# Gate and up products of three feed-forwards: both parts of h in one 512-column matmul, half results added by VectorE, the low part of the result on GpSimd

## The chip, the cores and the metric

One core of a Trainium2 chip runs the whole program. The metric is the device time of one execution in microseconds (us); the time of a kernel is the median of its runs.

## What is computed

Two blocks, each two layers deep, over 256 tokens of width 1024, in fp32. What matters here is the feed-forward of the first block. It comes four times (before and after the mixer of each of its two layers):

```python
def swiglu(h, w_gate, w_up, w_down):
    return (jax.nn.silu(h @ w_gate) * (h @ w_up)) @ w_down
...
x = x + 0.5 * swiglu(rms_norm(x, ffn2_norm[l]), ffn2_w_gate[l], ffn2_w_up[l], ffn2_w_down[l])
```

`w_gate` and `w_up` are 1024 x 2816, `w_down` is 2816 x 1024. The second block (retention, a gated unit, two products over 16384 experts) is not touched by the change.

## The kernel before

Everything is kept transposed: x is [128 partitions, 8 chunks of the 1024 features, 256 tokens]. Every product in fp32 is made of three products of fp32r numbers. Each operand is split into a high part and a low part (`h_hi`, `h_lo`; `w_hi`, `w_lo`), and high x high, high x low and low x high are added in PSUM by TensorE (`triple`, L620 to L623).

**Weights.** They stream from HBM in *units* of 128 x 1024, two to a load of 1 MB, into three buffers `raw` (SyncE, L2315). For each unit ScalarE writes `w_hi` (L1167) and VectorE writes `w_lo` = raw - `w_hi` (L1625). There are four buffers of each (`NPAIR`), so ScalarE may write unit n only once TensorE is done with unit n - 4, and SyncE may load only once VectorE has made the `w_lo` of three loads before. Between the pairs of units lie loads of `ada_w`; VectorE multiplies each half of these by a row and sums it (L1620), which TensorE doesn't need.

**The feed-forwards.** `FFN` lists four, c = 0 to 3. The loop over f = 0 to 21 takes 128 columns of gate (unit 2f) and of up (unit 2f + 1). A unit is 8 blocks of 128 x 128 weights, one for each chunk k of h. `project` does a block as one `triple`: three matmuls of 256 columns, into one half of a PSUM bank for gate and the other for up. For f = 0 of c > 0 `project_pairs` (L676 to L682) does the same in another order. Then, in order of the queues:

- VectorE, `ffn`: the `w_lo` of unit 2f + 4 (in `pair`); `activate(f - 1)`: it waits for Silu(f - 1), multiplies gate and up (L1771), waits for `a_hi`, and writes `a_lo` = product - `a_hi` (L1773); then it waits for unit 2f + 1 and scales both halves of the bank by the row `rr` into `sg` (L1794); then the `w_lo` of unit 2f + 5.
- ScalarE, `ffn`: the `w_hi` of unit 2f + 4; `a_split(f - 1)`: it waits for the product and copies it, rounded, to `a_hi` (L1243); the `w_hi` of unit 2f + 5; it waits for the scaling of f and takes Silu of the gate half in place (L1258).

The waits are semaphores, and each engine takes its instructions strictly in this order. `sg` has two buffers, used in turn by f.

**The down product** (`out_project`) has 176 blocks of weights. It uses `high_and_low` (L631, L632): one matmul of 512 columns takes `w_hi` against `a_hi` and `a_lo` side by side and leaves the low part's product in the bank's second half; one of 256 columns adds `w_lo` x `a_hi` to the first half. VectorE adds both halves to x (L1672, then, behind a wait for its own result, L1674). In c = 3 VectorE also works out rotary angles between the steps of f (L1738 to L1763). GpSimd adds squares of x for the next norm during the down products (`add_squares`, L2271 and L2275) and does nothing in the loops over f.

Of the kernel before, what the change touches and what calls it, by code (L numbers as in the profile page):

```python
# [17 lines left out]
T = 256  # L18
D = 1024
KT = 8  # L20
# [147 lines left out]
def build(nc, a, out):  # L168
    ctx = ExitStack()
    with ctx:  # L170
# [7 lines left out]
        hh_ = sb("h_hi", [128, KT, T], FR)  # L178
        hl_ = sb("h_lo", [128, KT, T], FR)
# [130 lines left out]
        silu_done = signal("silu_done", lambda c, f: 22 * c + f + 1)  # L310
# [125 lines left out]
        def out_after(c, key, K, m):  # L436
# [9 lines left out]
            "gu": lambda c, f: (gu_scaled, gu_scaled(c, f)),  # L446
            "out": lambda q, m: (x_upd, x_upd(q, m)),
# [169 lines left out]
        def _(e):  # L617
# [41 lines left out]

            def project_pairs(q, key, n, outs, lag=2, inside=None):  # L660

                for at in range(KT + lag * (len(outs) - 1)):
                    if at == inside:
                        added_sums(q)
                        sums(q, at, at)
                        sums(q, at + 1, at + 1)
                    for z, o in enumerate(outs):
                        k = at - lag * z
                        if not 0 <= k < KT:
                            continue  # L670
                        c = slice(k * 128, (k + 1) * 128)
                        w.wait_ge(h_hi, h_hi(q, k))
                        for half in range(2):
                            wh, wl = weights(unit[key, 2 * (n + z) + half])
                            s = slice(half * T, (half + 1) * T)
                            e.matmul(o[:, s], wh[:, c], by_halves(hh_[:, k, :]), start=k == 0 and half == 0, stop=False, skip_group_check=True)  # L676
                            e.matmul(o[:, s], wl[:, c], by_halves(hh_[:, k, :]), start=False, stop=False, skip_group_check=True)
                        w.wait_ge(h_lo, h_lo(q, k))
                        for half in range(2):
                            g = unit[key, 2 * (n + z) + half]  # L680
                            wh, wl = weights(g)
                            t = e.matmul(o[:, half * T:(half + 1) * T], wh[:, c], by_halves(hl_[:, k, :]), start=False, stop=k == KT - 1, skip_group_check=True)  # L682
                            if k == KT - 1:
                                t.then_inc(used.hit(g), 1)
# [91 lines left out]
            def ffn(c):  # L776
                which, l, q = FFN[c]
                for f in range(22):
# [4 lines left out]
                    if c == 0 and f == 14:  # L783
                        bias_tiles()
                    b = take(banks, ("gu", c, f))
# [12 lines left out]
                    if c > 0 and f == 1:  # L798
                        scale_row(q)
# [4 lines left out]
                    if c == 0 and f == 1:  # L804
                        for m in (4, 5):
                            sums(q, m, m)
                    if c == 0 and f == 2:
# [346 lines left out]
        def _(e):  # L1154
# [69 lines left out]
            def ffn(c, gains):  # L1224
# [20 lines left out]
                for f in range(22):  # L1245
# [8 lines left out]
                    if f >= 1:  # L1254
                        a_split(f - 1)
                    w_hi_upto(unit[(f"{which}_gu", l), 2 * f + 1] + 1 + NPAIR)
# [352 lines left out]
        def _(e):  # L1609
# [155 lines left out]
            def ffn(c, gains):  # L1765
# [3 lines left out]
                def activate(f):  # L1769
                    w.wait_ge(silu_done, silu_done(c, f))  # L1770
                    e.tensor_tensor(sg[f % 2][:, 0], sg[f % 2][:, 0], sg[f % 2][:, 1], ALU.mult).then_inc(gu_mul.hit(c, f), 1)  # L1771
                    w.wait_ge(a_hi_done, a_hi_done(c, f))
                    e.tensor_tensor(a_lo[:, f, :], sg[f % 2][:, 0], a_hi[:, f, :].bitcast(FP), ALU.subtract).then_inc(a_lo_done.hit(c, f), 1)  # L1773

                for f in range(22):
# [18 lines left out]
                    e.tensor_tensor(as_halves(sg[f % 2]), from_halves(bank["gu", c, f]), as_halves(one(rr).broadcast_to([128, 2, T])), ALU.mult).then_inc(gu_scaled.hit(c, f), 1)  # L1794
# [454 lines left out]
        def _(e):  # L2249
# [29 lines left out]

            for l in range(L):  # L2280
                add_squares(3 * l + 1)
# [4 lines left out]
                if l == 1:  # L2286
                    w.wait_ge(x_upd, x_upd(5, 7))
                    e.dma_start(dm, a["decay"]).then_inc(decay_in.sem, 16)
                    e.dma_start(posi, a["positions_2"].partition_broadcast(128)).then_inc(pos_in.sem, 16)
                add_squares(3 * l + 3)  # L2290
# [172 lines left out]
```

## Time and profile before

| | |
|---|---|
| Median of 3 runs | 2953.95 us (2953.05 to 2957.92) |
| The profiled execution | 2955.0 us, its span 2953.2 us |
| TensorE busy | 2919.2 us (99%) |
| TensorE weight loads | 2769.8 us (94%) |
| VectorE busy | 2204.2 us (75%) |
| ScalarE busy | 1605.8 us (54%) |
| GpSimd busy | 262.5 us (9%) |
| DMA, mean | 222 GB/s |

An engine is busy while an instruction runs on it; matmuls overlap each other, so the time that one takes is the distance between two starts and not its duration. The distance of starts is the measure on the other engines too, where the end of one instruction overlaps the next. The chain of waits runs over TensorE for 79% of the span, VectorE 10%, DMA 8%, ScalarE 2%.

### The profile page before, as it was taken

What the parts mean: (1) busy time and instruction counts of PE and PEld (TensorE: products, weight loads), DVE (VectorE), ACT (ScalarE), POOL (GpSimd) and SP (SyncE); (2) the same over time, 40 slices, a digit from 0 to 9 for tenths busy, and PEclk for the clock granted to TensorE, in tenths of its full rate; (3) what the DMA queues carried; (4) which work ended last, traced back from release to release, by engine and by line L of the source; (5) the groups of instructions that cost most, each with busy time, mean ns of one, the idle gap of its engine ahead of it and who ended that gap; (6) DMA issues with size and microseconds to landing.
All of it is one profiled execution on the core that took longest, in us unless ns stands there. A gap on an engine that the chain in (4) does not pass through costs nothing.

```text
span 2953.2 us, 51905 instructions
## 1 busy us (share of the span) xinstructions
PE 2919.2 (99%) x21818; PEld 2769.8 (94%) x21818; DVE 2204.2 (75%) x3531; ACT 1605.8 (54%) x2397; POOL 262.5 (9%) x233
## 2 busy tenths in 40 slices
PE   9999999999999999999999999999999999999999
PEld 9999999999999999999999998889999999999987
DVE  6887888886788847899755557776769986555676
ACT  5575655566544455556555555556545565555554
POOL 0010001010101102730000000000147000000000
PEclk9999999999999999999999999999999999999999
DMA  7773577775278555557876667655455688666673
GB/s 250 274 262 108 186 272 271 272 281 190 92 250 288 196 171 171 174 184 268 309 237 228 221 221 252 225 188 200 170 186 186 215 308 264 228 229 226 233 250 130
DMA packets 153688, 654.51 MB, mean 222 GB/s; under 512 B 10509, under 2 KB 77649, under 8 KB 78961
## 3 DMA queue, kind: packets, MB, share of 16 engines
q1 hardware_dynamic: 97744, 584.99, 57.0%
q10 hardware_dynamic: 55296, 64.76, 6.5%
q8 instruction: 173, 2.83, 0.4%
q0 software_dynamic: 416, 1.45, 0.1%
q14 instruction: 59, 0.48, 0.0%
HBM read 616.55 MB, written 34.61 MB: 220 GB/s over the span
## 4 chain that ended last, share of the span: by engine, by line
PE 79%; DVE 10%; DMA 8%; ACT 2%; issue 1%; DVEq 0%; ACTq 0%; SPq 0%
PE ps L621 12%; PE ps L622 12%; PE ps L623 12%; PE ps L626 8%; PE ps L628 8%; PE ps L627 8%; DMA gates<-at 6%; PE ps L631 6%; DVE w_lo L1625 3%; PE ps L632 3%; PE ps L823 2%; PE ps L697 1%; PE ps L698 1%; PE ps L700 1%; DVE raw L1620 1%; ACT w_hi L1167 1%
## 5 line engine op out<-in xcount | busy, mean ns | idle before, releaser
L1625 DVE TENSOR_TENSOR w_lo<-raw,w_hi 128x1024 fp32r<-128x1024 f32 x933 | 1140.9, 1232 | 497.2 <-ACT w_hi L1167 495.6
L1167 ACT ACTIVATE w_hi<-raw 128x1024 fp32r<-128x1024 f32 x1000 | 1048.1, 1056 | 575.2 <-PE ps L623 254.0
L621 PE MATMUL ps<-h_hi,w_hi 128*128 128x256 f32 x4240 | 1177.7, 278 | 6.2 <-DVE w_lo L1625 5.4
L622 PE MATMUL ps<-h_lo,w_hi 128*128 128x256 f32 x4240 | 1168.3, 276 | 0.0
L623 PE MATMUL ps<-h_hi,w_lo 128*128 128x256 f32 x4240 | 1168.2, 276 | 0.0
L621 PEld LDWEIGHTS ps<-h_hi,w_hi 128*128 128x128 f32 x4240 | 815.8, 192 | 12.2 <-issue 6.9
L622 PEld LDWEIGHTS ps<-h_lo,w_hi 128*128 128x128 f32 x4240 | 816.1, 192 | 2.0 <-issue 0.2
L623 PEld LDWEIGHTS ps<-h_hi,w_lo 128*128 128x128 f32 x4240 | 816.3, 193 | 0.0
L626 PE MATMUL ps<-w_hi,at 128*128 128x512 f32 x1024 | 388.4, 379 | 1.6 <-DVE at L2203 1.6
L627 PE MATMUL ps<-w_lo,at 128*128 128x512 f32 x1024 | 388.1, 379 | 0.0
L628 PE MATMUL ps<-w_hi,at 128*128 128x512 f32 x1024 | 388.1, 379 | 0.0
L631 PE MATMUL ps<-at,w_hi 128*128 128x512 f32 x832 | 273.2, 382 | 1.0 <-DVE at L1971 0.6
L632 PE MATMUL ps<-at,w_lo 128*128 128x256 f32 x832 | 226.8, 273 | 0.0
L626 PEld LDWEIGHTS ps<-w_hi,at 128*128 128x128 f32 x1024 | 193.7, 189 | 27.6 <-issue 1.9
L628 PEld LDWEIGHTS ps<-w_hi,at 128*128 128x128 f32 x1024 | 193.5, 189 | 27.4
L627 PEld LDWEIGHTS ps<-w_lo,at 128*128 128x128 f32 x1024 | 193.7, 189 | 25.8
L2271 POOL TENSOR_TENSOR tmp_h<-x 128x256 f32<-128x256 f32 x50 | 44.5, 890 | 1781.5 <-DVE x L1674 1658.0
L631 PEld LDWEIGHTS ps<-at,w_hi 128*128 128x128 f32 x832 | 157.3, 189 | 23.5 <-DVE at L1971 0.9
L2257 POOL TENSOR_TENSOR w_lo<-raw,w_hi 128x512 fp32r<-128x512 f32 x128 | 162.4, 1302 | 61.5 <-ACT w_hi L1167 61.3
L1489 ACT ACTIVATE at<-ps 128x512 f32<-128x512 f32 x128 | 76.8, 600 | 158.2 <-PE ps L623 158.1
L1560 ACT ACTIVATE at<-at 128x256 fp32r<-128x256 f32 x256 | 92.1, 409 | 126.6 <-DVE at L2199 126.6
L632 PEld LDWEIGHTS ps<-at,w_lo 128*128 128x128 f32 x832 | 159.7, 192 | 0.0
(292 smaller groups left out, 3223.2 us busy)
## 6 DMA issues: line engine op xcount, KB each, us to landing
raw<-in_peer_u SPq DMA_DIRECT2D x128, 1024.0 KB, 4.9
raw<-in_peer_v SPq DMA_DIRECT2D x128, 1024.0 KB, 4.9
raw<-in_ffn_gu SPq DMA_DIRECT2D x87, 1024.0 KB, 4.9
raw<-in_ada_w SPq DMA_DIRECT2D x48, 1024.0 KB, 5.1
raw<-in_ffn_down SPq DMA_DIRECT2D x44, 1024.0 KB, 4.9
gates<-at ACTq DMA_DIRECT2D x32, 1024.0 KB, 6.2
at<-gates ACTq DMA_DIRECT2D x24, 1024.0 KB, 6.3
raw<-in_w_in SPq DMA_DIRECT2D x16, 1024.0 KB, 4.9
```

Source lines behind the costliest of these rows:

```text
L621: e.matmul(o, lhs[0], rhs[0], start=start, stop=False)
L622: e.matmul(o, lhs[0], rhs[1], start=False, stop=False)
L623: return e.matmul(o, lhs[1], rhs[0], start=False, stop=stop)
L626: e.matmul(o, lhs[0], rhs[0], start=start, stop=False, skip_group_check=True)
L627: e.matmul(o, lhs[0], rhs[1], start=False, stop=False, skip_group_check=True)
L628: return e.matmul(o, lhs[1], rhs[0], start=False, stop=stop, skip_group_check=True)
L631: e.matmul(o, lhs[0], both.rearrange("p s (a b) -> p s b a", a=2), start=start, stop=False, skip_group_check=True)
L632: return e.matmul(o[:, 0:T], lhs[1], by_halves(both[:, 0]), start=False, stop=stop, skip_group_check=True)
L1167: e.activation(whi[:, u % NPAIR, :], raw(k, half), ACT.Copy).then_inc(hi_done.hit(u), 1)
L1560: e.activation(p_hi[k % 4], R[:, (2 * n) % NRING + e2, :], ACT.Copy).then_inc(p_hi_done.hit(l, k), 1)
L1625: e.tensor_tensor(wlo[:, m % NPAIR, :], raw(k, half), whi[:, m % NPAIR, :].bitcast(FP), ALU.subtract).then_inc(w_lo_dve.hit(m), 1)
L2257: t = e.tensor_tensor(wlo[:, n % NPAIR, c], raw(k, half)[:, c], whi[:, n % NPAIR, c].bitcast(FP), ALU.subtract)
```

## The change

In c = 1, 2 and 3, for f = 1 to 21, each block of a gate or up unit becomes a `high_and_low`: `w_hi` against the high and low parts of h at once (512 columns), then `w_lo` against the high part (256 columns). For that `h_hi` and `h_lo` lie in one tensor. Gate and up now take a bank each, of which the first half holds one partial sum and the second the other. ScalarE copies the first half of both banks to `sg`; VectorE waits for that, adds the second halves, waits for its own result and scales in SBUF. ScalarE's copies come behind `a_split(f - 1)` and wait for `a_lo` of f - 2. For the same three feed-forwards `a_lo` is made by GpSimd. c = 0 stays as it was.

```diff
--- before.py
+++ after.py
@@ -175,8 +175,8 @@
             return Signal(ctx.enter_context(nc.semaphore(name)), order)
 
         x = sb("x", [128, KT, T])
-        hh_ = sb("h_hi", [128, KT, T], FR)
-        hl_ = sb("h_lo", [128, KT, T], FR)
+        h_both = sb("h_hi_lo", [128, 2, KT, T], FR)
+        hh_, hl_ = h_both[:, 0], h_both[:, 1]
         sq = sb("sq", [128, 2, T])
         tmp_h = sb("tmp_h", [128, 3, T])
         ident = sb("ident", [128, 128])
@@ -307,7 +307,11 @@
         rows_half = signal("rows_half", lambda r: r + 1)
 
         gu_scaled = signal("gu_scaled", lambda c, f: 22 * c + f + 1)
-        silu_done = signal("silu_done", lambda c, f: 22 * c + f + 1)
+        def gu_scalar(c, f, copied=False):
+
+            return f + 1 if c == 0 else 22 + 43 * (c - 1) + 2 * f + (not copied)
+
+        silu_done = signal("silu_done", gu_scalar)
         gu_mul = signal("gu_mul", lambda c, f: 22 * c + f + 1)
         a_hi_done = signal("a_hi_done", lambda c, f: 22 * c + f + 1)
         a_lo_done = signal("a_lo_done", lambda c, f: 22 * c + f + 1)
@@ -444,6 +448,7 @@
 
         evacuated = {
             "gu": lambda c, f: (gu_scaled, gu_scaled(c, f)),
+            "gj": lambda c, f, z: (gu_scaled, gu_scaled(c, f)),
             "out": lambda q, m: (x_upd, x_upd(q, m)),
             "hook": lambda n: (hook_free, hook_free(n)),
             "lam": lambda: (lam_exp, 1),
@@ -657,6 +662,14 @@
                     t = triple(o, (wh[:, c], wl[:, c]), h_part(k), k == 0, k == KT - 1)
                 t.then_inc(used.hit(n), 1)
 
+            def project_high_and_low(q, n, o):
+                wh, wl = weights(n)
+                for k in range(KT):
+                    c = slice(k * 128, (k + 1) * 128)
+                    w.wait_ge(h_lo, h_lo(q, k))
+                    t = high_and_low(o, (wh[:, c], wl[:, c]), h_both[:, :, k, :], k == 0, k == KT - 1)
+                t.then_inc(used.hit(n), 1)
+
             def project_pairs(q, key, n, outs, lag=2, inside=None):
 
                 for at in range(KT + lag * (len(outs) - 1)):
@@ -782,6 +795,13 @@
                         lambdas()
                     if c == 0 and f == 14:
                         bias_tiles()
+                    if c > 0 and f > 0:
+                        for z in range(2):
+                            b = take(banks, ("gj", c, f, z))
+                            project_high_and_low(q, unit[(f"{which}_gu", l), 2 * f + z], b)
+                            if f == 1 and z == 0:
+                                scale_row(q)
+                        continue
                     b = take(banks, ("gu", c, f))
                     if f == 0:
                         if c == 0:
@@ -795,16 +815,14 @@
                             sums(q, m, m)
                         continue
                     project(q, unit[(f"{which}_gu", l), 2 * f], b[:, 0:T])
-                    if c > 0 and f == 1:
-                        scale_row(q)
                     if c == 0 and f < 3:
                         for m in (4 * f - 2, 4 * f - 1):
                             sums(q, m, m)
                     project(q, unit[(f"{which}_gu", l), 2 * f + 1], b[:, T:2 * T])
-                    if c == 0 and f == 1:
+                    if f == 1:
                         for m in (4, 5):
                             sums(q, m, m)
-                    if c == 0 and f == 2:
+                    if f == 2:
                         scale_row(q)
                 out_project(q + 1, (f"{which}_down", l), 22, lambda i: a_hl[:, :, i, :],
                             lambda i: (a_lo_done, a_lo_done(c, i)), c, last=c == 3)
@@ -1253,6 +1271,13 @@
                     pair((f"{which}_gu", l), f)
                     if f >= 1:
                         a_split(f - 1)
+                    if c > 0 and f > 0:
+                        if f > 1:
+                            w.wait_ge(a_lo_done, a_lo_done(c, f - 2))
+                        for z in range(2):
+                            w.wait_ge(*unit_after((f"{which}_gu", l), 2 * f + z))
+                            t = e.activation(as_halves(sg[f % 2][:, z:z + 1]), from_halves(bank["gj", c, f, z][:, 0:T]), ACT.Copy)
+                        t.then_inc(silu_done.hit(c, f, True), 1)
                     w_hi_upto(unit[(f"{which}_gu", l), 2 * f + 1] + 1 + NPAIR)
                     w.wait_ge(gu_scaled, gu_scaled(c, f))
                     e.activation(sg[f % 2][:, 0], sg[f % 2][:, 0], ACT.Silu).then_inc(silu_done.hit(c, f), 1)
@@ -1769,8 +1794,9 @@
                 def activate(f):
                     w.wait_ge(silu_done, silu_done(c, f))
                     e.tensor_tensor(sg[f % 2][:, 0], sg[f % 2][:, 0], sg[f % 2][:, 1], ALU.mult).then_inc(gu_mul.hit(c, f), 1)
-                    w.wait_ge(a_hi_done, a_hi_done(c, f))
-                    e.tensor_tensor(a_lo[:, f, :], sg[f % 2][:, 0], a_hi[:, f, :].bitcast(FP), ALU.subtract).then_inc(a_lo_done.hit(c, f), 1)
+                    if c == 0:
+                        w.wait_ge(a_hi_done, a_hi_done(c, f))
+                        e.tensor_tensor(a_lo[:, f, :], sg[f % 2][:, 0], a_hi[:, f, :].bitcast(FP), ALU.subtract).then_inc(a_lo_done.hit(c, f), 1)
 
                 for f in range(22):
                     if c == 0 and f == 8:
@@ -1791,7 +1817,16 @@
                     if f == 0:
                         w_lo_upto(unit[(f"{which}_gu", l), 1 if c > 0 else 5] + 1 + NPAIR)
                         w.wait_ge(rr_ready, rr_ready(q))
-                    e.tensor_tensor(as_halves(sg[f % 2]), from_halves(bank["gu", c, f]), as_halves(one(rr).broadcast_to([128, 2, T])), ALU.mult).then_inc(gu_scaled.hit(c, f), 1)
+                    if c > 0 and f > 0:
+                        w.wait_ge(silu_done, silu_done(c, f, True))
+                        for z in range(2):
+                            both = as_halves(sg[f % 2][:, z:z + 1])
+                            t = e.tensor_tensor(both, both, from_halves(bank["gj", c, f, z][:, T:2 * T]), ALU.add)
+                        step(t)
+                        stepped()
+                        e.tensor_tensor(sg[f % 2], sg[f % 2], one(rr).broadcast_to([128, 2, T]), ALU.mult).then_inc(gu_scaled.hit(c, f), 1)
+                    else:
+                        e.tensor_tensor(as_halves(sg[f % 2]), from_halves(bank["gu", c, f]), as_halves(one(rr).broadcast_to([128, 2, T])), ALU.mult).then_inc(gu_scaled.hit(c, f), 1)
                     if c == 0 and f == 4:
                         bias_rows()
                     w_lo_upto(unit[(f"{which}_gu", l), 2 * f + 1] + 1 + NPAIR)
@@ -2277,7 +2312,14 @@
                             t.then_inc(pool_step.hit(), 1)
                 t.then_inc(sq_added.hit(q), 1)
 
+            def a_split(c):
+                for f in range(22):
+                    w.wait_ge(a_hi_done, a_hi_done(c, f))
+                    e.tensor_tensor(a_lo[:, f, :], sg[f % 2][:, 0], a_hi[:, f, :].bitcast(FP), ALU.subtract).then_inc(a_lo_done.hit(c, f), 1)
+
             for l in range(L):
+                if l == 1:
+                    a_split(2)
                 add_squares(3 * l + 1)
                 w.wait_ge(qk_inv, qk_inv(l))
                 e.tensor_copy(mrx[:, 2:4].rearrange("p i t z (m d) -> p (i t z m) d", m=2),
@@ -2287,6 +2329,7 @@
                     w.wait_ge(x_upd, x_upd(5, 7))
                     e.dma_start(dm, a["decay"]).then_inc(decay_in.sem, 16)
                     e.dma_start(posi, a["positions_2"].partition_broadcast(128)).then_inc(pos_in.sem, 16)
+                a_split(2 * l + 1)
                 add_squares(3 * l + 3)
             add_squares(7)
             peer(0)
```

## Rows read from the trace of the kernel before

**Rows 1.** Busy time by stage: stretch, length, each engine's busy us, PEclk, DMA share, GB/s.

```profile
332.00:445.00 113.00, 113.00 (x1004) 112.69 (x1003) 96.69 (x139) 60.26 (x86) 0.00 (x0) 1.00 0.76 271
...
509.00:622.00 113.00, 113.00 (x1003) 112.68 (x1002) 98.69 (x142) 60.08 (x86) 0.00 (x0) 1.00 0.76 278
...
809.00:927.00 118.00, 116.34 (x1013) 114.77 (x1012) 102.71 (x158) 60.34 (x88) 0.00 (x0) 1.00 0.73 261
```

**Rows 2.** VectorE in order of time, c = 1: start us, us, instruction [idle before].

```profile
378.87 0.68 DVE L1794 TENSOR_TENSOR at<-ps,rr 128x512 f32<-128x512 f32 x1
...
380.99 1.23 DVE L1625 TENSOR_TENSOR w_lo<-raw,w_hi 128x1024 fp32r<-128x1024 f32 x1 [0.28 <-ACT w_hi L1167]
382.13 0.42 DVE L1771 TENSOR_TENSOR at<-at 128x256 f32<-128x256 f32 x1
383.04 0.42 DVE L1773 TENSOR_TENSOR at<-at,at 128x256 fp32r<-128x256 f32 x1 [0.49 <-ACT at L1243]
383.38 0.68 DVE L1794 TENSOR_TENSOR at<-ps,rr 128x512 f32<-128x512 f32 x1
...
389.81 0.68 DVE L1794 TENSOR_TENSOR at<-ps,rr 128x512 f32<-128x512 f32 x1
```

**Rows 3.** VectorE: first and last scaling of c = 1, and w_lo of unit 48.

```profile
332.11 0.69 DVE L1794 TENSOR_TENSOR at<-ps,rr 128x512 f32<-128x512 f32 x1
...
443.41 0.68 DVE L1794 TENSOR_TENSOR at<-ps,rr 128x512 f32<-128x512 f32 x1
...
447.02 1.23 DVE L1625 TENSOR_TENSOR w_lo<-raw,w_hi 128x1024 fp32r<-128x1024 f32 x1 [0.53 <-ACT w_hi L1167]
```

**Rows 4.** TensorE in order of time: four blocks of c = 1; first and next-stage start of down.

```profile
380.10 0.28 PE L621 MATMUL ps<-h_hi,w_hi 128*128 128x256 f32 x1
...
381.44 0.28 PE L621 MATMUL ps<-h_hi,w_hi 128*128 128x256 f32 x1
...
441.07 0.38 PE L631 MATMUL ps<-at,w_hi 128*128 128x512 f32 x1
...
498.71 0.28 PE L676 MATMUL ps<-h_hi,w_hi 128*128 128x256 f32 x1
```

**Rows 5.** ScalarE in order of time, the same turn of c = 1.

```profile
379.59 0.42 ACT L1258 ACTIVATE at<-at 128x256 f32<-128x256 f32 x1
379.92 1.04 ACT L1167 ACTIVATE w_hi<-raw 128x1024 fp32r<-128x1024 f32 x1
382.58 0.42 ACT L1243 ACTIVATE at<-at 128x256 fp32r<-128x256 f32 x1 [1.63 <-DVE at L1771]
```

**Rows 6.** Waits of TensorE in c = 3: us in total, times, longest us.

```profile
PE ps L621 <- DVE w_lo L1625: 1.7, 3, 0.9
```

**Rows 7.** Down product of c = 3, in order of time: VectorE, then TensorE.

```profile
941.01 1.23 DVE L1625 TENSOR_TENSOR w_lo<-raw,w_hi 128x1024 fp32r<-128x1024 f32 x1 [1.18 <-ACT w_hi L1167]
...
942.29 0.48 PE L631 MATMUL ps<-at,w_hi 128*128 128x512 f32 x1
```

**Rows 8.** Groups of ScalarE by line and shape: busy us, mean ns | idle before.

```profile
L1313 ACT ACTIVATE at<-ps,cols 128x256 f32<-128x256 f32 x16 | 6.7, 471 | 0.0
```

**Rows 9.** ScalarE in order of time, in the mixer: two copies out of PSUM.

```profile
240.09 0.83 ACT L1313 ACTIVATE at<-ps,cols 128x256 f32<-128x256 f32 x2
```

**Rows 10.** VectorE in order of time: an operation and the one that needs its result.

```profile
471.43 0.41 DVE L1672 SCALAR_TENSOR_TENSOR x<-ps,x 128x256 f32<-128x256 f32 x1
471.88 0.42 DVE L1674 SCALAR_TENSOR_TENSOR x<-ps,x 128x256 f32<-128x256 f32 x1
```

**Rows 11.** In order of time: GpSimd undisturbed; VectorE beside GpSimd's operation of 473.99.

```profile
450.25 0.61 POOL L2271 TENSOR_TENSOR tmp_h<-x 128x256 f32<-128x256 f32 x1 [128.15 <-DVE x L1674]
...
474.12 1.75 DVE L1625 TENSOR_TENSOR w_lo<-raw,w_hi 128x1024 fp32r<-128x1024 f32 x1
```

**Rows 12.** VectorE in order of time: a turn in which the load was late.

```profile
392.74 1.23 DVE L1625 TENSOR_TENSOR w_lo<-raw,w_hi 128x1024 fp32r<-128x1024 f32 x1 [1.10 <-ACT w_hi L1167]
```

**Rows 13.** Busy time of one stretch of c = 3, columns as in rows 1.

```profile
848.00:863.00 15.00, 13.34 (x111) 12.50 (x110) 13.41 (x24) 6.58 (x11) 0.00 (x0) 1.00 0.73 255
```

## The prediction

> **What bounds the kernel now.** I read first the busy time and the granted clock of the three feed-forward stretches that the change touches, then single instructions in order of time on each engine inside one of them.
>
> In the gate and up stretches of feed-forwards c = 1, 2 and 3 TensorE is busy 113.00 of 113, 113.00 of 113 and 116.34 of 118 us, at the full clock (1.00, the 2.4 GHz level) [rows 1]. That alone would say that every nanosecond taken from TensorE shows in the time. The rows of VectorE say otherwise. Look at one turn of the loop over f, from one scaling of the pair of products (L1794) to the next. It takes 4.51 us (378.87 to 383.38), and 6.43 us where two sums over `ada_w` lie in it (383.38 to 389.81) [rows 2]. In c = 1 the 21 turns take 443.41 - 332.11 = 111.30 us, 5.30 us each [rows 3]. TensorE's two units of a turn are 16 blocks; four blocks take 381.44 - 380.10 = 1.34 us, so 0.335 us a block and 5.36 us a turn [rows 4]. So the two loops run neck and neck.
>
> What makes up VectorE's 4.51 us? In none of these turns does VectorE wait for TensorE: its two waits are 0.28 us for ScalarE's `w_hi` and 0.49 us for ScalarE's `a_hi` (L1243) [rows 2]. ScalarE in turn waits 1.63 us for VectorE's product of gate and up (L1771), and starts its `w_hi` right behind the Silu (L1258) [rows 5]. This is a closed ring between two in-order queues:
>
> scaling(f) starts; 0.72 later Silu(f) (378.87, 379.59); 0.33 later `w_hi` (379.92); 1.07 later `w_lo` (380.99); 1.14 later the product (382.13); 0.45 later `a_hi` (382.58); 0.46 later `a_lo` (L1773, 383.04); 0.34 later scaling(f+1) (383.38). The sum is 4.51 [rows 2, 5].
>
> The ring is hidden only because it leads TensorE by the four weight buffers. At the end of c = 1 its lead is: unit 48 of the stage is needed at 441.07 + 4 x 8 x 0.3275 = 451.55 and its `w_lo` ends at 447.02 + 1.23 = 448.25, so 3.3 us [rows 3, 4]. In c = 3, where rotary angles share VectorE, there is none: TensorE waits 1.7 us for `w_lo` [rows 6], and in its down product one `w_lo` ends at 941.01 + 1.23 = 942.24 and the TensorE block that starts behind it at 942.29 takes 0.48 us where its like takes 0.38: it had to wait a little there too [rows 4, 7].
>
> **The change, part by part.** It acts on f = 1 to 21 of c = 1, 2, 3: 63 turns, 126 units, 1008 blocks.
>
> *TensorE.* Three products of 256 columns become one of 512 and one of 256; the columns stay 768. The down product already has the new form: 176 blocks in 498.71 - 441.07 = 57.64 us, 0.3275 us each [rows 4]. Gain 0.335 - 0.3275 = 0.0075 us a block, 1008 x 0.0075 = 7.6 us, if nothing else binds. The Trainium skill (TensorE: Matmul & The Clock Gate, Back-to-back issue gap) gives columns / 2.4 GHz plus 2.5 ns for each matmul; by that estimate one matmul less saves only 2.5 ns a block, 2.5 us in all.
>
> *ScalarE.* Two copies of 128x256 out of PSUM a turn. They stand in its queue behind a_split(f-1), which waits for VectorE's product of f-1, and their signal comes after the second. So they don't run ahead while TensorE works: they join the ring. Nearest rows: one copy PSUM to SBUF of that size takes 0.47 us [rows 8], two in a row 0.83 together, so they start 0.36 apart [rows 9]. Behind them stands `w_hi` of unit 2f+5; it ends 1.4 us after the second copy starts, VectorE wants it 1.9 us after, so it costs nothing; if the data came later, it would.
>
> *VectorE.* `a_lo` and its wait for `a_hi` go (0.46 + 0.34 of the ring). It now waits for both copies, then adds twice (0.34 apart, as L1773 and what follows it, 383.04 to 383.38 [rows 2]), waits for its own second add, and scales from SBUF at the same size as before. For add to dependent operation I take L1672 to L1674, 471.43 to 471.88: 0.45 [rows 10]. Behind the waiting add are queued the scaling, both next `w_lo` and, where they fall, the `ada_w` sums; Silu and TensorE wait for these.
>
> *The new ring.* Up to the start of `a_hi` it stays 4.51 - 0.46 - 0.34 = 3.71. Then: 0.33 to the first copy (as from Silu, of the same size, to what follows it), 0.36 to the second, 0.47 + 0.03 to the first add, 0.34 to the second, 0.45 to the scaling: 1.98. New turn 5.69, against 4.51: **1.18 more**. With copies of 0.40 and an own wait of 0.40 it would be 1.05; I take 1.15. Turns with `ada_w` sums grow by the same, since their extra work lies ahead of the product: 6.43 to 7.58. The mean becomes 5.30 + 1.15 = 6.45 us, against 5.24 that TensorE would need (16 x 0.3275). TensorE starves, and its own gain is worth nothing.
>
> *GpSimd.* An operation of that size on it takes 0.61 us when undisturbed [rows 11]. `a_lo` starts behind `a_hi`, when VectorE is idle for 1.2 us waiting for the copies, and ends just before the first add; ScalarE asks for it only two turns later. At the end TensorE wants a_lo(21) 21 blocks (6.9 us) into the down product. Its queue holds `add_squares` of the next down product behind it, whose data come later. Cost nothing while the idle stretch covers it. Without that cover: beside a GpSimd operation a `w_lo` of VectorE took 1.75 us instead of 1.23 [rows 2, 11]. By the Trainium skill (GPSIMD Engine Reference, Key points) the two share SBUF interfaces, above all with VectorE instructions of two SBUF inputs; the adds have one input in PSUM, the `w_lo` and the scaling have two in SBUF.
>
> *DMA.* No transfer is added or moved. Loads wait for `w_lo`, so they come later, with the ring. A few turns wait for a load (1.10 us before one `w_lo`, and its turn is 0.8 longer than 4.51 for it [rows 12]); a slower ring hides these: I take 0.95 us for c = 1 (this one and a small one) and 0.8 for c = 2.
>
> *The sum.* 63 x 1.15 = 72.5; less hidden load waits 1.8; less the lead that is used up first, 3.3 in c = 1, about the same in c = 2, which repeats it, none in c = 3: 72.5 - 1.8 - 6.6 = 64 us. The profiled execution took 2955.0 us (span 2953.2), so 3019. The median of the three runs is 1.05 us lower: **3018**. Bounds of the unknown pieces: 63 x 1.0 gives +55, 63 x 1.3 gives +74.
>
> **The rivals.**
>
> *A, faster:* the copies are taken as each unit ends and hide behind TensorE, so that TensorE binds. Place: the copy after `a_hi` in ScalarE's queue. Price: 7.6 us gained, 2946. It needs a ring that grows by less than about 0.1 us a turn (5.36 - 5.30, and the lead of 3.3 us spread over 21 turns gives 0.15 more). For it: ScalarE and VectorE each have idle time in every turn. Against: that idle time is made of waits inside the ring [rows 2, 5]. The skill's 2.5 us in place of 7.6 would only make it 2951.
>
> *B, slower still by GpSimd:* its `a_lo` falls on VectorE's adds or `w_lo` and costs 0.5 us a turn (1.75 - 1.23 [rows 11]): 63 x 0.5 = 32 more, 3050. Against: the idle stretch is 1.2 us long. In part, 3030 to 3040.
>
> *C, less:* pieces overlap that I put in line (a copy starting earlier, PSUM read faster): ring +0.6, 63 x 0.6 - 8 = 30, 2984.
>
> *D, the clock:* TensorE idle for a fifth of each turn, and the granted clock falls to the 1.2 GHz level. A block then takes twice 0.3275, a turn 10.5 us, 4.0 more than the ring: 63 x 4.0 = 250 more, 3270. Against: in 848 to 863, where TensorE was busy 13.34 of 15 us, the clock was 1.00 [rows 13]. The Trainium skill (TensorE: Matmul & The Clock Gate, HAM oscillation) describes kernels whose clock drops with repeated waits; the trace shows no such drop here.
>
> **How the numbers follow.** 0.2% (6 us) is about what a measurement of this kernel can tell. Forecast 0.70 (3006 to 3030); A 0.05; B wholly or in part 0.14; C 0.08; D 0.03. Range: 3000 to 3048, which leaves out A, C's lower half, full B's top and D. Faster 0.05, same 0.02, slower 0.93.
>
> **What would show it.** Right: turns of about 5.7 and 7.6 us; VectorE idle some 1.2 us before its adds, put down to the ScalarE copies; ScalarE's two copies 0.36 apart right behind `a_hi`; TensorE waiting for `w_lo` in nearly every turn of c = 1, 2 and 3 after the first four or so; GpSimd operations near 0.6 us; stretches of some 132 to 138 us where 113 to 118 stood. Wrong: no TensorE waits for `w_lo` (then A), VectorE operations longer beside GpSimd (B), a clock below 1.00 (D), or a growth outside these three stretches.

## The result, and the profile after

The changed kernel takes 3020.16 us (median of 4 runs, 3018.31 to 3022.4) against 2953.5 us: a ratio of 1.0226, interval [1.0213, 1.0239], 66.7 us slower. The forecast was 3018.

The page of the changed kernel first: span, busy time by engine, the chain that ended last by engine.

```profile
span 3017.3 us, 50211 instructions
...
PE 2930.9 (97%) x20810; PEld 2733.3 (91%) x20810; DVE 2227.8 (74%) x3591; ACT 1636.3 (54%) x2523; POOL 307.8 (10%) x299
...
PE 71%; DVE 18%; DMA 6%; ACT 3%; issue 1%; SPq 0%; POOL 0%; DVEq 0%; ACTq 0%
```

TensorE has 1008 instructions fewer and the chain that ended last runs over VectorE for 18% instead of 10%. VectorE is busy for only 24 us more over the whole span and for a smaller share of it. Shares of busy time would not have told that the loop now hangs on it.

The same three stages by busy time (stretch, length, busy us of each engine, PEclk, DMA share, GB/s), which answer to [rows 1]:

```profile
328.00:456.00 128.00, 115.75 (x676) 101.17 (x675) 98.88 (x149) 68.70 (x126) 14.38 (x20) 1.00 0.62 226
527.00:655.00 128.00, 115.96 (x676) 101.37 (x676) 101.12 (x153) 68.52 (x124) 14.60 (x20) 1.00 0.63 232
850.00:985.00 135.00, 118.23 (x676) 102.45 (x676) 106.61 (x171) 69.32 (x128) 14.36 (x20) 0.99 0.62 224
```

Where 113, 113 and 118 us were needed and TensorE had next to no gap, it now stands idle for 12 to 17 us of each stage (stretches of 128, 128 and 135 us), at nearly the clock of before. VectorE in order of time, one turn without `ada_w` sums and the first half of one with them (start us, us, instruction, idle before and its releaser). L1796 is the product, L1824 the two adds, L1827 the scaling, L1650 `w_lo`:

```profile
387.68 0.69 DVE L1827 TENSOR_TENSOR at<-at,rr 128x512 f32<-128x512 f32 x1
388.28 1.22 DVE L1650 TENSOR_TENSOR w_lo<-raw,w_hi 128x1024 fp32r<-128x1024 f32 x1
389.80 1.23 DVE L1650 TENSOR_TENSOR w_lo<-raw,w_hi 128x1024 fp32r<-128x1024 f32 x1 [0.29 <-ACT w_hi L1185]
390.94 0.42 DVE L1796 TENSOR_TENSOR at<-at 128x256 f32<-128x256 f32 x1
392.45 0.75 DVE L1824 TENSOR_TENSOR at<-at,ps 128x256 f32<-128x256 f32 x2 [1.10 <-PE ps L637]
393.24 0.69 DVE L1827 TENSOR_TENSOR at<-at,rr 128x512 f32<-128x512 f32 x1
...
400.72 0.69 DVE L1827 TENSOR_TENSOR at<-at,rr 128x512 f32<-128x512 f32 x1
```

The turn takes 393.24 - 387.68 = 5.56 us (4.51 before) and 400.72 - 393.24 = 7.48 (6.43 before). The idle 1.10 us before the adds is new. In this turn the profile puts it down to TensorE's L637, in others to ScalarE's copies. ScalarE's rows show which it is, since `a_hi` (L1261), the two copies (L1279) and the next `w_hi` follow each other without a gap, the first released by VectorE's product:

```profile
391.39 0.42 ACT L1261 ACTIVATE at<-at 128x256 fp32r<-128x256 f32 x1 [1.63 <-DVE at L1796]
391.71 0.64 ACT L1279 ACTIVATE at<-ps 128x256 f32<-128x256 f32 x2
392.24 1.06 ACT L1185 ACTIVATE w_hi<-raw 128x1024 fp32r<-128x1024 f32 x1
```

What TensorE waited for from the first unit of c = 1 to the end of its down product (us in total, times, longest us):

```profile
PE ps L636 <- DVE w_lo L1650: 12.3, 15, 1.1
PE ps L636 <- POOL at L2318: 3.4, 1, 3.4
```

These waits are not all. Right behind the last one the granted clock fell. The first line is that stretch of the changed kernel, the second the stretch behind the same wait in the kernel with narrow matmuls (the first experiment below):

```profile
467.90:471.00 3.10, 3.10 (x10) 2.65 (x11) 3.02 (x4) 0.96 (x2) 0.00 (x0) 0.50 0.70 293
```

```profile
468.50:472.00 3.50, 3.48 (x21) 3.22 (x22) 3.12 (x4) 1.24 (x3) 0.12 (x1) 1.00 0.69 274
```

At 0.50, the 1.2 GHz level, the blocks of the down product start 0.64 us apart instead of 0.3275, here in c = 2:

```profile
667.40 0.64 PE L636 MATMUL ps<-at,w_hi 128*128 128x512 f32 x1
...
668.04 0.64 PE L636 MATMUL ps<-at,w_hi 128*128 128x512 f32 x1
```

The down products of c = 1, 2 and 3 each have such a stretch, of 3.4, 6.8 and 3.4 us; those of the kernel before have none. From the block that waits (the 22nd) to the start of the last they took 52.31, 53.59 and 52.42 us, against 50.65, 50.65 and 50.80 before: 6.2 us in all.

From the first unit to the end of the down product c = 1 grew by 22 us, c = 2 by 23, c = 3 by 24. The rest of the span is some 5 us shorter, which is no effect of the change: from the last down product to the end the profiled executions of the kernels below lie between 1970 and 1981 us, in no order that follows their edits.

### The profile page after: what moved, and what is told of

It reads as the page before. It is cut to its first block, busy times and chain, and to the rows that moved or that the text cites. A ratio compares the mean times of both kernels' runs of the same rounds, so it can differ in the third digit from the quotient of the medians.

```text
span 3017.3 us, 50211 instructions
## 1 busy us (share of the span) xinstructions
PE 2930.9 (97%) x20810; PEld 2733.3 (91%) x20810; DVE 2227.8 (74%) x3591; ACT 1636.3 (54%) x2523; POOL 307.8 (10%) x299
## 4 chain that ended last, share of the span: by engine, by line
PE 71%; DVE 18%; DMA 6%; ACT 3%; issue 1%; SPq 0%; POOL 0%; DVEq 0%; ACTq 0%
PE ps L626 9%; PE ps L628 9%; PE ps L627 9%; PE ps L631 8%; PE ps L636 8%; PE ps L633 8%; PE ps L632 8%; DVE w_lo L1650 6%; DMA gates<-at 5%; PE ps L637 4%; DVE raw L1645 2%; PE ps L841 2%; DVE at L1824 2%; DVE at L1827 1%; PE ps L710 1%; PE ps L711 1%
## 5 line engine op out<-in xcount | busy, mean ns | idle before, releaser
L1650 DVE TENSOR_TENSOR w_lo<-raw,w_hi 128x1024 fp32r<-128x1024 f32 x933 | 1140.0, 1231 | 500.4 <-ACT w_hi L1185 498.4
L626 PE MATMUL ps<-h_hi_lo,w_hi 128*128 128x256 f32 x3232 | 897.1, 278 | 4.3 <-DVE w_lo L1650 3.8
L627 PE MATMUL ps<-h_hi_lo,w_hi 128*128 128x256 f32 x3232 | 888.8, 275 | 0.0
L628 PE MATMUL ps<-h_hi_lo,w_lo 128*128 128x256 f32 x3232 | 888.8, 275 | 0.0
L626 PEld LDWEIGHTS ps<-h_hi_lo,w_hi 128*128 128x128 f32 x3232 | 620.1, 192 | 9.4 <-issue 5.2
L627 PEld LDWEIGHTS ps<-h_hi_lo,w_hi 128*128 128x128 f32 x3232 | 620.3, 192 | 2.0 <-issue 0.2
L628 PEld LDWEIGHTS ps<-h_hi_lo,w_lo 128*128 128x128 f32 x3232 | 620.5, 192 | 0.0
L636 PE MATMUL ps<-h_hi_lo,w_hi 128*128 128x512 f32 x1008 | 342.8, 390 | 41.1 <-DVE w_lo L1650 39.6
L636 PE MATMUL ps<-at,w_hi 128*128 128x512 f32 x832 | 280.6, 389 | 12.7 <-POOL at L2318 10.0
L637 PE MATMUL ps<-h_hi_lo,w_lo 128*128 128x256 f32 x1008 | 275.5, 273 | 0.0
L636 PEld LDWEIGHTS ps<-h_hi_lo,w_hi 128*128 128x128 f32 x1008 | 191.1, 190 | 85.9 <-DVE w_lo L1650 40.8
L637 PE MATMUL ps<-at,w_lo 128*128 128x256 f32 x832 | 229.5, 276 | 0.0
L637 PEld LDWEIGHTS ps<-h_hi_lo,w_lo 128*128 128x128 f32 x1008 | 194.0, 193 | 0.0
```

The costliest lines, as they stand in the source:

```text
L626: e.matmul(o, lhs[0], rhs[0], start=start, stop=False)
L627: e.matmul(o, lhs[0], rhs[1], start=False, stop=False)
L628: return e.matmul(o, lhs[1], rhs[0], start=False, stop=stop)
L636: e.matmul(o, lhs[0], both.rearrange("p s (a b) -> p s b a", a=2), start=start, stop=False, skip_group_check=True)
L637: return e.matmul(o[:, 0:T], lhs[1], by_halves(both[:, 0]), start=False, stop=stop, skip_group_check=True)
L1650: e.tensor_tensor(wlo[:, m % NPAIR, :], raw(k, half), whi[:, m % NPAIR, :].bitcast(FP), ALU.subtract).then_inc(w_lo_dve.hit(m), 1)
```

## The experiments

All differ from the changed kernel or from each other by one part. Each was run beside the kernel before on the same chip.

### Narrow matmuls, all else as changed

```diff
-                    t = high_and_low(o, (wh[:, c], wl[:, c]), h_both[:, :, k, :], k == 0, k == KT - 1)
+                    hi, lo = h_part(k)
+                    e.matmul(o[:, 0:T], wh[:, c], hi, start=k == 0, stop=False, skip_group_check=True)
+                    e.matmul(o[:, T:2 * T], wh[:, c], lo, start=False, stop=False, skip_group_check=True)
+                    t = e.matmul(o[:, 0:T], wl[:, c], hi, start=False, stop=k == KT - 1, skip_group_check=True)
```

> The changed kernel with three matmuls of 256 columns a block in place of one of 512 and one of 256; both banks, the copies and the adds stay. Ring theory (the turn of ScalarE and VectorE sets the time, 5.56 us without and 7.48 us with ada_w sums): TensorE then needs 5.36 us a turn instead of 5.24, both below the ring's mean of about 6.3, so the time stays at 3020, within 3 us, and TensorE only waits less. Rival (TensorE's form itself costs the time, by wide matmuls that start late or disturb each other): most of the 67 us goes back, 2953 to 2975.

Measured: 3021.74 us, ratio 1.0237 [1.0216, 1.0258]. The same as the changed kernel: the wide matmul itself neither costs nor gives anything there. TensorE's waits for `w_lo` in c = 1 fell only from 12.3 to 10.3 us:

```profile
PE ps L671 <- DVE w_lo L1653: 10.3, 14, 1.0
```

In c = 1 of this run TensorE waits 3.4 us for the last `a_lo` as in the changed kernel, and the clock stays at 1.00 behind it. The stage grew by 20.6 us there, where it grew by 22.0 in the changed kernel, so the fall of the clock is worth 1.5 us in c = 1. Why it fell in one of the two and not in the other isn't shown.

### a_lo back on VectorE

```diff
                 def activate(f):
...
-                    if c == 0:
-                        w.wait_ge(a_hi_done, a_hi_done(c, f))
-                        e.tensor_tensor(a_lo[:, f, :], sg[f % 2][:, 0], a_hi[:, f, :].bitcast(FP), ALU.subtract).then_inc(a_lo_done.hit(c, f), 1)
+                    w.wait_ge(a_hi_done, a_hi_done(c, f))
+                    e.tensor_tensor(a_lo[:, f, :], sg[f % 2][:, 0], a_hi[:, f, :].bitcast(FP), ALU.subtract).then_inc(a_lo_done.hit(c, f), 1)
```

(GpSimd's two `a_split` calls go.)

> The changed kernel with a_lo of c = 1 to 3 back on VectorE. Ring theory: VectorE has about 1.1 us of idle time between the product and the adds, in which a_hi ends after about 0.9 and a_lo (0.34) fits before the copies are done; the turn stays near 5.56 and the time near 3020. A little less, by 1 us or so, since the last a_lo of each stage comes some 0.3 us earlier and TensorE waits 3.4, 3.5 and 3.1 us for it at the 22nd block of the down product. Rival (moving a_lo to GpSimd is what keeps the change from being worse still, each a_lo on VectorE is worth its 0.34 us in the ring): 63 x 0.34 = 21 more, 3041.

Measured: 3020.05 us, ratio 1.023 [1.0213, 1.0247]. The same again, so `a_lo` on GpSimd takes nothing off the path. VectorE in order of time shows why: `a_lo` (L1798) lies in the idle stretch, and 0.19 us of waiting for the copies is still left behind it. The turn is 394.04 - 388.47 = 5.57.

```profile
388.47 0.69 DVE L1826 TENSOR_TENSOR at<-at,rr 128x512 f32<-128x512 f32 x1
...
391.73 0.42 DVE L1796 TENSOR_TENSOR at<-at 128x256 f32<-128x256 f32 x1
392.63 0.42 DVE L1798 TENSOR_TENSOR at<-at,at 128x256 fp32r<-128x256 f32 x1 [0.48 <-ACT at L1261]
393.25 0.75 DVE L1823 TENSOR_TENSOR at<-at,ps 128x256 f32<-128x256 f32 x2 [0.19 <-PE ps L637]
394.04 0.69 DVE L1826 TENSOR_TENSOR at<-at,rr 128x512 f32<-128x512 f32 x1
```

### Two more copies in each turn

```diff
                             w.wait_ge(*unit_after((f"{which}_gu", l), 2 * f + z))
+                            e.activation(as_halves(spare[f % 2][:, z:z + 1]), from_halves(bank["gj", c, f, z][:, 0:T]), ACT.Copy)
                             t = e.activation(as_halves(sg[f % 2][:, z:z + 1]), from_halves(bank["gj", c, f, z][:, 0:T]), ACT.Copy)
```

> The changed kernel with two further ScalarE copies in each turn: each first half is also copied to a spare tile that nobody reads, right ahead of the copy that counts. It prices the copies. Ring theory: 0.26 us for each further copy (two in 0.64 us in the trace of the changed kernel), so 0.52 x 63 = 33 us more, 3053. Rival (the copies wait for nothing that matters; the adds or GpSimd make the loss): 3020, since ScalarE is idle over 3 us in each turn.

Measured: 3058.49 us, ratio 1.0351 [1.0336, 1.0366], 38 us more than the changed kernel. The turn went from 5.56 to 399.12 - 393.00 = 6.12:

```profile
393.00 0.69 DVE L1829 TENSOR_TENSOR at<-at,rr 128x512 f32<-128x512 f32 x1
...
396.26 0.42 DVE L1798 TENSOR_TENSOR at<-at 128x256 f32<-128x256 f32 x1
398.33 0.75 DVE L1826 TENSOR_TENSOR at<-at,ps 128x256 f32<-128x256 f32 x2 [1.65 <-ACT at L1281]
399.12 0.69 DVE L1829 TENSOR_TENSOR at<-at,rr 128x512 f32<-128x512 f32 x1
```

0.56 x 63 = 35 us, and in the profiled executions the three feed-forwards take 34.8 us longer. The copies are paid in full, one for one, although ScalarE is idle for over a third of the turn.

### The copies ahead of a_split

The same instructions in another order on ScalarE:

```diff
-                    if f >= 1:
-                        a_split(f - 1)
                     if c > 0 and f > 0:
...
                         t.then_inc(silu_done.hit(c, f, True), 1)
+                    if f >= 1:
+                        a_split(f - 1)
```

> The changed kernel with ScalarE's two copies of f ahead of a_split(f - 1) in its queue; the work is the same. Ring theory: the copies then run while VectorE makes the second w_lo and leave the ring, which becomes 3.26 to the product, 0.34 + 0.34 + 0.45 to the scaling, about 4.4 to 4.5 us a turn and 6.3 with ada_w sums, mean 5.2, no more than TensorE's 5.24. TensorE binds again, and its own gain of 7.6 us shows, with some of the waits of c = 3 gone: 2943 to 2950. Rival (the added work itself is too much for ScalarE and VectorE, wherever it stands): stays above 3000. A second rival: the copies now wait for unit 2f + 1 and hold up a_hi and the next w_hi behind them, so that part is lost: 2955 to 2985.

Measured: 2973.49 us, ratio 1.0067 [1.005, 1.0084]. This gives back 47 of the 67 us, with no work taken away, so the position in the queue is what the copies cost. But it fell 23 us or more short of what I expected, and into the range of my second rival. That rival's mechanism is not what the rows show: `a_hi` starts 0.45 us behind the product (385.47 behind 385.02), as before. VectorE and GpSimd in order of time:

```profile
385.02 0.42 DVE L1796 TENSOR_TENSOR at<-at 128x256 f32<-128x256 f32 x1
385.35 0.75 DVE L1824 TENSOR_TENSOR at<-at,ps 128x256 f32<-128x256 f32 x2
386.13 1.10 DVE L1827 TENSOR_TENSOR at<-at,rr 128x512 f32<-128x512 f32 x1
387.16 1.21 DVE L1650 TENSOR_TENSOR w_lo<-raw,w_hi 128x1024 fp32r<-128x1024 f32 x1
...
385.96 0.73 POOL L2318 TENSOR_TENSOR at<-at,at 128x256 fp32r<-128x256 f32 x1 [4.07 <-ACT at L1261]
```

Product, adds and scaling now follow each other without a wait, as expected. But the scaling takes 1.10 us instead of 0.69, and GpSimd's `a_lo` (385.96 to 386.69) runs into it. The two adds take their usual 0.75, but only the last 0.14 us of them lies beside it. The idle stretch that had covered `a_lo` on GpSimd is gone, and the disturbance that the prediction priced for that case appears, on the scaling. The turn was 4.80 and 6.70 us. That GpSimd is the cause is tried in two of the experiments below.

The longer turns are not all that is left. TensorE still waits 2 to 3 us for the last `a_lo` of each down product, and behind two of these waits the clock is at its lower level again (6.8 us in c = 1, 3.4 us in c = 2, none in c = 3). The down products of c = 1 and 2 took 3.0 and 1.5 us more for it.

### a_lo late on VectorE

On top of the kernel with the copies first, `a_lo(f - 1)` leaves GpSimd and comes behind the `w_lo` of unit 2f + 5:

```diff
                     w_lo_upto(unit[(f"{which}_gu", l), 2 * f + 1] + 1 + NPAIR)
+                    if c > 0 and f > 0:
+                        low(f - 1)
                 activate(21)
+                if c > 0:
+                    low(21)
```

> Copies first, as in the run before, and a_lo of c = 1 to 3 back on VectorE, but late: a_lo(f - 1) behind the w_lo of unit 2f + 5, where VectorE is idle 0.30 us for w_hi. In the run with the copies first the scaling took 1.11 us beside GpSimd's a_lo and 0.69 without it, so the turn was 4.80 us and 6.70 with ada_w sums. Theory (GpSimd's a_lo beside the scaling is what was left of the loss): turns of about 4.42 and 6.64, mean (13 x 4.42 + 8 x 6.64) / 21 = 5.27, close to TensorE's 5.24: 2946 to 2955. Rival (the added adds and copies are themselves too much, GpSimd's disturbance hides behind other waits): 2970 or more.

Measured: 2957.24 us, ratio 1.0008 [0.9999, 1.0017]. Another 16 us are back, some 4 of them because the clock does not fall in any of the down products. The scaling is at 0.69 us again with both its inputs in SBUF, now that GpSimd is idle in the loop:

```profile
L1830 DVE TENSOR_TENSOR at<-at,rr 128x512 f32<-128x512 f32 x63 | 43.6, 692 | 2.2
```

Turns are 4.46 us, but those with `ada_w` sums 6.76; the means over the 21 turns are 5.44, 5.37 and 5.64 us in c = 1, 2 and 3, still above the 5.24 of TensorE.

### The same with narrow matmuls

The edit is that of the first experiment, on top of the kernel just shown.

> The kernel of e5_a_lo_late with three matmuls of 256 columns a block instead of one of 512 and one of 256, everything else as there. It prices the wide matmul by itself. If TensorE binds in e5, the narrow form costs 1008 x 0.0075 = 7.6 us more than e5 by the rows of before; by the 2.5 ns a matmul of the Trainium skill it would be 2.5 us. If the ring still binds in e5 (mean 5.27 and above), part of this is hidden: 0 to 4 us.

Measured: 2961.01 us, ratio 1.0019 [1.0011, 1.0028]: 3.8 us more than with wide matmuls. The intervals of the two runs overlap, and the three feed-forwards of the two profiled executions differ by 0.7 us. So less than the 7.6 us shows here, as expected while VectorE is still slightly the bound; how much less can't be told.

### a_lo on GpSimd alone

The kernel before, with `a_lo` of c = 1 to 3 made by GpSimd as in the change, and a wait for it ahead of the scaling:

```diff
+                    if c > 0 and f > 1:
+                        w.wait_ge(a_lo_done, a_lo_done(c, f - 2))
                     e.tensor_tensor(as_halves(sg[f % 2]), from_halves(bank["gu", c, f]), as_halves(one(rr).broadcast_to([128, 2, T])), ALU.mult).then_inc(gu_scaled.hit(c, f), 1)
```

> The kernel before with one part of the change alone: a_lo of c = 1 to 3 on GpSimd (the scaling of f waits for a_lo of f - 2). Ring theory: the ring loses 0.46 + 0.34 us and becomes 3.6 to 4.1 us a turn, by how much GpSimd disturbs the scaling or a w_lo; TensorE binds everywhere, and the waits of c = 3 go (its stage took 116.39 us where the others took 113.09): 3 to 5 us gained, 2948 to 2951. Rival (GpSimd's disturbance of VectorE costs more than the 0.80 it takes away): 2955 to 2975.

Measured: 2953.88 us, ratio 0.9997 [0.9988, 1.0006]. No gain. VectorE's shortest turns did fall, to 4.25 and 4.34 us from 4.51, but TensorE's own work set the time in c = 1 already, and in c = 3 it still waited 1.3 us for `w_lo`, where 1.7 stood before [rows 6]. Set matmul beside matmul, the gate and up products of c = 3 fall behind those of c = 1 at three such waits and at the block starts that follow them, and nowhere else that counts: by 3.3 us before and by 2.8 here. So the 3 us that c = 3 takes longer are VectorE's, but `a_lo` is not what holds it up. The waits lie among the turns with rotary angles, and turns of 8.01, 5.71, 7.28 and 6.03 us before are 8.00, 5.71, 7.28 and 6.04 here. VectorE waits no longer for `a_hi`, but 0.84 us for the `w_hi` that stands behind `a_hi` in ScalarE's queue. This is the turn of 6.04 us:

```profile
849.44 0.68 DVE L1797 TENSOR_TENSOR at<-ps,rr 128x512 f32<-128x512 f32 x1
850.96 1.23 DVE L1625 TENSOR_TENSOR w_lo<-raw,w_hi 128x1024 fp32r<-128x1024 f32 x1 [0.84 <-ACT w_hi L1167]
```

### The scaling row from PSUM

On top of the kernel with the copies first (and `a_lo` on GpSimd), one operand changes. The row of scales stands in PSUM anyway; ScalarE's copy of it in SBUF is no longer read here:

```diff
-                        e.tensor_tensor(sg[f % 2], sg[f % 2], one(rr).broadcast_to([128, 2, T]), ALU.mult).then_inc(gu_scaled.hit(c, f), 1)
+                        e.tensor_tensor(sg[f % 2], sg[f % 2], one(sum_bank[:, 128:384]).broadcast_to([128, 2, T]), ALU.mult).then_inc(gu_scaled.hit(c, f), 1)
```

> The kernel of e3_copies_first (copies ahead of a_split, a_lo on GpSimd) with the scaling row read from PSUM, where it already stands, instead of SBUF, so that the scaling has one SBUF input. In e3 the scaling took 1.11 us beside GpSimd's a_lo, in the kernel with a_lo late 0.69; the two adds beside it, with one input in PSUM, took their usual 0.75. Theory (GpSimd delays only VectorE instructions with two SBUF inputs): the scaling goes back to 0.69, turns 4.38 and 6.28 us, mean (13 x 4.38 + 8 x 6.28) / 21 = 5.10, below TensorE's 5.24: TensorE binds, the wait for the last a_lo at the 22nd block of the down product goes too, and the wide matmul's gain shows: 2944 to 2951. Rival (any VectorE instruction beside GpSimd is delayed): as e3, 2973.

Measured: **2947.09 us**, ratio 0.9978 [0.9968, 0.9988]. This is faster than both kernels, than the one before by 0.2%, which is small but clear of the noise. VectorE and GpSimd in order of time:

```profile
381.32 0.69 DVE L1827 TENSOR_TENSOR at<-at,ps 128x512 f32<-128x512 f32 x1
...
386.97 0.74 DVE L1824 TENSOR_TENSOR at<-at,ps 128x256 f32<-128x256 f32 x2
387.74 0.69 DVE L1827 TENSOR_TENSOR at<-at,ps 128x512 f32<-128x512 f32 x1
...
392.12 0.69 DVE L1827 TENSOR_TENSOR at<-at,ps 128x512 f32<-128x512 f32 x1
...
387.57 0.73 POOL L2318 TENSOR_TENSOR at<-at,at 128x256 fp32r<-128x256 f32 x1 [5.68 <-ACT at L1261]
```

The scaling lies wholly beside GpSimd's `a_lo` and takes 0.69. The turn is 6.42 us with `ada_w` sums (381.32 to 387.74) and 4.38 without (387.74 to 392.12), as expected within 0.14. The clock does not fall in any of the three down products. TensorE is busy 112.00 of 112 us in c = 1:

```profile
325.00:437.00 112.00, 112.00 (x691) 103.07 (x691) 104.29 (x156) 74.33 (x129) 14.75 (x20) 1.00 0.72 265
```

### The same with narrow matmuls

The first experiment's edit once more, on this kernel.

> The kernel of e8_row_in_psum with three matmuls of 256 columns a block instead of one of 512 and one of 256. It prices the wide matmul where TensorE binds. By the rows of before 1008 x 0.0075 = 7.6 us slower than e8, so 2952 to 2958. By the Trainium skill's 2.5 ns a matmul 2.5 us slower. If VectorE still binds in e8 (as in e5, where the narrow form cost 3.8), less than 4.

Measured: 2954.68 us, ratio 1.0 [0.9992, 1.0009], so 7.6 us more than with the wide matmul. That is what the two rates of the kernel before gave, 1008 x 0.0075 us, but the two ratios leave some 4 us to either side. The traces are sharper where TensorE alone sets the time: the gate and up products of c = 1 took 118.51 us with the wide matmul and 121.04 with narrow ones, 2.53 us for 336 blocks, so 0.0075 each. Over the three feed-forwards it is 5.5 us, because in c = 2 and 3 the faster kernel still waits 0.4 and 0.8 us for the last `a_lo`, and in c = 3 for `w_lo`.

## Why the prediction was right

*The ring, confirmed.* The step that decided was that ScalarE's copies stand behind `a_split(f - 1)` and so join the closed ring of ScalarE and VectorE. Doubling the copies costs their full time, moving them out of the ring gives most of the loss back, and the form of the matmuls makes no difference while the ring binds. Rival A (the copies hide) is out for this order of the queue and right for the other one. D is out as the cause of the loss, since the clock was at 1.00 and 0.99 in the stretches of gate and up. It is not out altogether. The lower level came, for 3.4 to 6.8 us in each of the three down products, and took 6.2 us of the 66.7. The prediction had looked at one stretch of c = 3 alone [rows 13]; just behind the down product of c = 3, from 981.5 to 984.9, the kernel before had been at the lower level too.

*The size of the ring's growth.* I took 1.15 us from a worked-out 1.18 and it was 1.05 (4.51 to 5.56, 6.43 to 7.48). Up to `a_hi` it is 3.71 (387.68 to 391.39), as worked out. One term was too large: first copy to first add is 0.74, not 0.86 (391.71 to 392.45), and most of that is that the copies start 0.26 apart, not 0.36 (two in 0.64 us, where I had rows of 0.83 for copies with a scale from a column). The adds and the scaling took 0.79, as predicted (0.34 + 0.45).

*The lead, taken at the wrong place.* With 63 x 1.05 = 66 us in place of 72.5, less 1.8 and 6.6, the sum would have been 58 and not 64. It came out at 66.7, and the three feed-forwards grew by 22, 23 and 24 us. I had taken the lead where TensorE needs the `w_lo` of unit 48, 3.3 us. But it needs the last `a_lo`, of f = 21, sooner, at the 22nd block: in c = 1 before at 441.07 + 21 x 0.3275 = 447.95. That `a_lo` ended at 446.06 + 0.42 = 446.48, so the lead was 1.5 us there:

```profile
446.06 0.42 DVE L1773 TENSOR_TENSOR at<-at,at 128x256 fp32r<-128x256 f32 x1 [0.48 <-ACT at L1243]
```

I had costed this `a_lo` at nothing, by the 6.9 us that TensorE takes to its block. That cover is there only as long as the ring keeps its lead. In the changed kernel TensorE waits 3.4 us there, where the last `a_lo` on GpSimd ends at 467.05 + 0.73:

```profile
467.83 0.80 PE L636 MATMUL ps<-at,w_hi 128*128 128x512 f32 x1 [3.45 <-POOL at L2318]
```

The wait has nearly the same size in c = 2 and c = 3 (3.5 and 3.1 us). That GpSimd makes this `a_lo` is not its cause: with `a_lo` on VectorE it was 3.4, 3.4 and 2.3 us.

*How the 66.7 us come about.* In c = 1 the 21 turns grew by 132.78 - 111.30 = 21.5 us, since 0.6 us of late loads was hidden. The last `a_lo` comes 0.35 us later behind its scaling, and 1.5 us of lead comes off. That gives the 20.4 us by which the 22nd block of the down product comes later. The clock adds 1.7 behind it: 22. In the same way c = 2 is 20.2 and 2.9, and c = 3, which had next to no lead, 22.6 and 1.6. The three together are 63.2 us, the clock 6.2, and the rest of the span was 5 us shorter: 64 us between the two profiled spans, 66.7 between the medians.

So the ring was priced 6 us too high, 5 us too much was taken off for lead and loads, and the clock's 6 us were left out. The first error cancels about half of the other two. That the total came out within some 2 us of the forecast was partly luck.

*GpSimd.* The cover held: its `a_lo` starts in the idle 1.10 us and, at 0.73 us instead of 0.61, ends 0.17 us behind the start of the adds (391.89 + 0.73 against 392.45); adds and scaling keep 0.75 and 0.69. Its price without cover is real. 0.41 us a turn were seen, near the 0.5 of rival B, but only once the copies were moved.

*TensorE's gain.* 7.6 us, hidden in the changed kernel and measured as 7.6 where TensorE binds. The Trainium skill (TensorE: Matmul & The Clock Gate, Back-to-back issue gap) gives 2.5 ns for a matmul beyond its columns; by that estimate one matmul less a block was worth 2.5 us, and the 7.5 ns a block measured in c = 1 is three times that.

## What to carry to other kernels

Ahead of adding work to an engine with much idle time, add up the turn of the loop across the engines: start to start, from an instruction back to itself, through each queue and each wait. If the idle time is waiting inside that ring, every added instruction in it counts in full, and the cure is its place in the queue; here the same instructions in another order took 47 us less. Where an engine runs ahead by its buffers, ask for every consumer of its results how large the lead is there, since it is used up first at the narrowest of them. Behind each long wait of TensorE read the clock in a stretch of a few us; the mean of a whole stage hides a fall of 3 us.

## What was not expected of the hardware

VectorE's delay beside GpSimd hung on where its operands lie. The scaling of 128x512 took 1.10 us with both inputs in SBUF and 0.69 with one of them in PSUM, each beside the same GpSimd operation of 0.73 us. The mean over 63 scalings was 1114 ns (copies first) against 687 (row in PSUM):

```profile
L1827 DVE TENSOR_TENSOR at<-at,rr 128x512 f32<-128x512 f32 x63 | 70.2, 1114 | 2.2
```

```profile
L1827 DVE TENSOR_TENSOR at<-at,ps 128x512 f32<-128x512 f32 x63 | 43.3, 687 | 2.2
```

The Trainium skill (GPSIMD Engine Reference, Key points) says that the two engines contend where the VectorE instruction has two SBUF inputs; both rows agree. I had cited it in the prediction, and not thought of moving an operand to where it doesn't hold. That one operand is the 26 us between 2973.49 and 2947.09: by the length of the turns, by the shorter waits for the last `a_lo`, and by some 4 us of lower clock that no longer come. With the order of the copies it makes the change a gain of 0.2%.
